# A two-direction gated recurrence: two score buffers, the output products moved behind the next tile's second group, and both directions' outputs in the same banks

## The reference

```python
S_t = diag(f_t) S_{t-1} + k_t v_t^T
o_t = S_t^T q_t
o   = o_forward + flip(o_backward)      # then an RMS norm for each head
```

## Time and profile before

| | |
|---|---|
| median of 3 runs | 4069.83 us (4064.1 to 4074.27) |
| the profiled execution | 4068.36 us |
| its span in the trace | 4066.5 us, mean granted PE clock 0.955 |
| PE busy | 3695.6 us, 91% of the span |
| DVE, ACT, POOL busy | 2607.3, 2022.8, 1042.4 us |

### The profile page before, as it was taken

The page is one execution under the profiler, slowest core; times in us unless marked ns, Lnnn a source line. Parts: engine busy times, 40 slices in busy tenths (PEclk is TensorE's granted clock), DMA queues, the critical chain, the costliest instruction groups (busy, mean ns, idle before and its releaser), DMA issues. The chain is left out here.

```text
span 4066.5 us, 57429 instructions
## 1 busy us (share of the span) xinstructions
PE 3695.6 (91%) x21576; PEld 2898.5 (71%) x21576; DVE 2607.3 (64%) x3794; ACT 2022.8 (50%) x3880; POOL 1042.4 (26%) x1106
## 2 busy tenths in 40 slices
PE   6999898888999787888789999999898989999998
PEld 5775677777775676767466666678666768888886
DVE  3766567767765486776555555548966776665655
ACT  4544366655544286655344444456644554444444
POOL 0016103732017003610155555500281010111000
PEclk7989899999989898999899999999999999999999
DMA  5100113345200102351100000122003551111344
GB/s 192 42 16 1 39 52 112 129 154 189 69 21 1 54 21 99 119 182 54 31 5 7 9 6 6 36 81 80 9 5 138 189 154 42 60 44 42 110 155 150
DMA packets 211397, 295.44 MB, mean 73 GB/s; under 512 B 74218, under 2 KB 140010, under 8 KB 211124
## 3 DMA queue, kind: packets, MB, share of 16 engines
q1 hardware_dynamic: 210564, 291.57, 21.6%
q0 software_dynamic: 416, 0.05, 0.0%
q10 hardware_dynamic: 144, 0.15, 0.0%
HBM read 261.12 MB, written 30.51 MB: 72 GB/s over the span
## 5 line engine op out<-in xcount | busy, mean ns | idle before, releaser
L563 DVE TENSOR_TENSOR x_low<-buf_a,x_high 128x640 fp32r<-128x640 f32 (+5 forms) x360 | 359.9, 1000 | 307.3 <-ACT x_high L610 290.2
L610 ACT CAST x_high<-buf_a 128x640 fp32r<-128x640 f32 (+5 forms) x360 | 311.0, 864 | 394.8 <-PE ps L670 322.2
L668 PE MATMUL ps<-x_high,w_high 128*128 128x512 f32 (+1 forms) x1184 | 443.4, 375 | 61.5 <-DVE w_low L567 55.9
L669 PE MATMUL ps<-x_low,w_high 128*128 128x512 f32 (+1 forms) x1184 | 436.9, 369 | 0.0
L670 PE MATMUL ps<-x_high,w_low 128*128 128x512 f32 (+1 forms) x1184 | 436.0, 368 | 0.0
L3321 PE MATMUL ps<-w_high,x_high 128*128 128x512 f32 x896 | 362.4, 404 | 53.9 <-DVE w_low L3170 52.0
L3322 PE MATMUL ps<-w_low,x_high 128*128 128x512 f32 x896 | 356.1, 397 | 0.0
L3323 PE MATMUL ps<-w_high,x_low 128*128 128x512 f32 x896 | 355.7, 397 | 0.0
L3170 DVE TENSOR_TENSOR w_low<-w,w_high 128x1024 fp32r<-128x1024 f32 x170 | 226.4, 1332 | 172.7 <-ACT w_high L3262 172.7
L3905 DVE TENSOR_REDUCE mx<-ps 128x1 fp32r<-128x1280 f32 x128 | 190.7, 1491 | 200.2 <-PE ps L3780 199.7
L668 PEld LDWEIGHTS ps<-x_high,w_high 128*128 128x128 f32 x1184 | 226.6, 191 | 109.7 <-DVE x_low L563 64.6
(11 more groups left out here) (451 smaller groups left out, 8910.9 us busy)
## 6 DMA issues: line engine op xcount, KB each, us to landing
w<-in_w_out SPq DMA_DIRECT2D x26, 2048.0 KB, 8.4
w<-in_w_mod SPq DMA_DIRECT2D x24, 2048.0 KB, 9.1
w<-in_w_down SPq DMA_DIRECT2D x15, 2048.0 KB, 7.9
w<-in_w_in SPq DMA_DIRECT2D x26, 1024.0 KB, 5.2
w<-in_w_up SPq DMA_DIRECT2D x22, 1024.0 KB, 7.6
w<-in_w_in SPq DMA_DIRECT2D x6, 2048.0 KB, 8.8
x<-in_x SPq DMA_DIRECT2D x16, 512.0 KB, 8.9
scratch_h<-x SPq DMA_DIRECT2D x8, 512.0 KB
```

The lines of the kernel that those rows point to most:

```text
L563: dve.tensor_tensor(part(xl, i)[:, 0:s["tn"]], x_of(s), part(xh, i)[:, 0:s["tn"]].bitcast(F32), ALU.subtract).then_inc(x_low, 1)
L610: act.copy(part(xh, i)[:, 0:s["tn"]], x_of(s)).then_inc(x_high, 1)
L668: pe.matmul(g["out"], lhs[0][:, :], rhs[0][:, :], start=(s["kk"] == 0), stop=False)
L669: pe.matmul(g["out"], lhs[0][:, :], rhs[1][:, :], start=False, stop=False)
```

## The change

- `sc` becomes two buffers for each direction, taken in turn by tile. `place` then waits only for the output product of two tiles ago. Two more buffers are cleared at the start.
- The four blocks of outputs get columns of their own for each direction in banks 6 and 7 (`r.out`). The first direction's first product alone carries `start`. The two directions' output products no longer wait for each other, but both readers (`first_output`, `output`) wait for the products of both directions, and the next tile's products wait for both readers.
- On PE `outputs_of(r, u-1)` moves from ahead of group 0 to behind group 1 of the same direction. Turned keys and state products come after both directions' level products.
- On DVE `output` moves from group 0 to the end of group 2, and `state` behind both directions' copies of group 1.
- On ACT `first_output` moves to the end of group 1, `squares` from group 2 to group 3, and the first modulation copy-out from the end of the tile to the end of group 2. Both `place` come ahead of both `keys_out`.

```diff
@@ scalar
-                act.wait_ge(r.o_ready, j) if j else act.wait_ge(r.zeroed, 2)
+                act.wait_ge(r.o_ready, j - 1) if j >= 2 else act.wait_ge(r.zeroed, 3)
...
-                act.wait_ge(r.o_ready, n_out[u] + 1)
+                for w in D2:
+                    act.wait_ge(w.o_ready, n_out[u] + 1)
...
                     for r in D2:
                         if g == 0:
-                            if u:
-                                first_output(r, u - 1)
                             place(r, u)
+                    for r in D2:
+                        if g == 0:
                             keys_out(r, u)
                         if g == 1 and u + 1 < NU:
                             exponentials(r, u + 1)
                         if first <= u < NU - 1:
                             level_exponentials(r, u + 1, g)
-                        if g == 2 and u:
+                        if g == 1 and u:
+                            first_output(r, u - 1)
+                        if g == G - 1 and u:
                             squares(r, u - 1)
-                for j in mods_at.get(u, ()):
+                    if g == 2:
+                        for j in mods_at.get(u, ())[:1]:
+                            mods.evacuate(act, mods.first + j)
+                for j in mods_at.get(u, ())[1:]:
                     mods.evacuate(act, mods.first + j)
@@ vector
                     for r in D2:
-                        if g == 0 and n_out[u]:
-                            output(r, u - 1)
                         copies(r, u, g)
                         if g == 0:
                             scale_levels(r, u, G - 1)
                         elif u + 1 < NU:
                             scale_levels(r, u + 1, g - 1)
+                    for r in D2:
                         if g == 1:
                             state(r, u)
+                        if g == 2 and n_out[u]:
+                            output(r, u - 1)
@@ tensor
-                if r is D2[1]:
-                    pe.wait_ge(D2[0].o_out, j + 1)
-                elif j:
+                if r is D2[0] and j:
+                    pe.wait_ge(D2[0].o_out, j)
                     pe.wait_ge(D2[1].o_out, j)
...
                     for r in D2:
-                        if g == 0 and n_out[u]:
+                        level_products(r, u, g)
+                        if g == 1 and n_out[u]:
                             outputs_of(r, u - 1)
-                        level_products(r, u, g)
+                    for r in D2:
                         if g == 0:
                             turn_keys(r, u)
                         if g == 1:
                             states(r, u)
@@ Scan
-        self.sc = lay("sc" + n, [P, 2, 2, P])
+        self.sc = [lay(f"sc{n}{i}", [P, 2, 2, P]) for i in range(2)]
+        self.out = slice(direction * P, (direction + 1) * P)
```

More of the change, by code:

```diff
@@ L1094, in place @@
                 act.wait_ge(r.products, G * j + 1)
-                act.wait_ge(r.o_ready, j) if j else act.wait_ge(r.zeroed, 2)
-                to = r.sc[:, :, :, :].rearrange("p a c t -> p (a c) t")
+                act.wait_ge(r.o_ready, j - 1) if j >= 2 else act.wait_ge(r.zeroed, 3)
+                to = r.sc[j % 2][:, :, :, :].rearrange("p a c t -> p (a c) t")
                 heads = ps[:, r.bank:r.bank + 2, :].rearrange("p a (c x) -> p (a c) x", c=2)
@@ L1117, in first_output @@
                     return
-                act.wait_ge(r.o_ready, n_out[u] + 1)
-                src = ps[:, 6:8, 0:P].rearrange("p a (c e) -> p a c e", c=2)
+                for w in D2:
+                    act.wait_ge(w.o_ready, n_out[u] + 1)
+                src = ps[:, 6:8, r.out].rearrange("p a (c e) -> p a c e", c=2)
                 act.copy(o[:, r.order[u], :].rearrange("p (c a e) -> p a c e", c=2, a=2), src).then_inc(r.o_out, 1)
@@ L1211, in output @@
                 j, t = n_out[u], r.order[u]
-                dve.wait_ge(r.o_ready, j + 1)
-                src = ps[:, 6:8, 0:P].rearrange("p a (c e) -> p a c e", c=2)
+                for w in D2:
+                    dve.wait_ge(w.o_ready, j + 1)
+                src = ps[:, 6:8, r.out].rearrange("p a (c e) -> p a c e", c=2)
                 dst = o[:, t, :].rearrange("p (c a e) -> p a c e", c=2, a=2)
@@ L1220, in _ @@
             for r in D2:
-                dve.memset(r.sc[:, :, :, :], 0.0).then_inc(r.zeroed, 1)
+                for sc in r.sc:
+                    dve.memset(sc[:, :, :, :], 0.0).then_inc(r.zeroed, 1)
                 dve.memset(r.S[0][:, :, :], 0.0).then_inc(r.zeroed, 1)
-                dve.wait_ge(r.zeroed, 2)
+                dve.wait_ge(r.zeroed, 3)
             for r in D2:
@@ L1291, in outputs_of @@
                 pe.wait_ge(r.qe_scaled, j + 1)
-                if r is D2[1]:
-                    pe.wait_ge(D2[0].o_out, j + 1)
-                elif j:
+                if r is D2[0] and j:
+                    pe.wait_ge(D2[0].o_out, j)
                     pe.wait_ge(D2[1].o_out, j)
                 for h in range(4):
-                    c, out = h // 2, ps[:, 6 + h % 2, h // 2 * HD:(h // 2 + 1) * HD]
-                    pe.matmul(out, r.sc[:, h % 2, c, :], v[:, t, h * HD:(h + 1) * HD], start=(c == 0), stop=False,
-                              skip_group_check=True)
+                    c, out = h // 2, ps[:, 6 + h % 2, r.out.start + h // 2 * HD:r.out.start + (h // 2 + 1) * HD]
+                    pe.matmul(out, r.sc[j % 2][:, h % 2, c, :], v[:, t, h * HD:(h + 1) * HD],
+                              start=(c == 0 and r is D2[0]), stop=False, skip_group_check=True)
                 for h in range(4):
-                    c, p0, out = h // 2, (h % 2) * HD, ps[:, 6 + h % 2, h // 2 * HD:(h // 2 + 1) * HD]
+                    c, p0 = h // 2, (h % 2) * HD
+                    out = ps[:, 6 + h % 2, r.out.start + h // 2 * HD:r.out.start + (h // 2 + 1) * HD]
                     mm = pe.matmul(out, r.qe[j % 2][p0:p0 + HD, c, :], r.S[u % 2][p0:p0 + HD, c, :], start=False,
@@ L1495, in mixer_layer @@
     mods.begin(*MODS_IN[layer], lambda j: 4 + j % 2, Layout(k, A_B, A_B + 4 * T * 4), BR + P)
-    recurrence(k, qk, a, v, o, (stat, junk), range(nt0, NT), Layout(k, A_A, A_B), mods)
+    recurrence(k, qk, a, v, o, (stat, junk), range(nt0, NT), Rooms(Layout(k, A_A, A_B), lay), mods)
     return RecurrenceNorm(k, layer, o, stat, YT, nt0, Layout(k, A_A, A_B),
```

## The result

| | median of the runs | the profiled execution, its span | ratio to before, 95% interval |
|---|---|---|---|
| before, 20 runs | 4067.77 us (4059.33 to 4078.48) | 4068.36, 4066.5 us | |
| changed, 20 runs | 4077.31 us (4072.53 to 4091.51) | 4074.3, 4072.5 us | 1.0029 [1.0019, 1.0039] |

The forecast was 4086 us, 16 above the median then known. Measured are 9.5 us by the two medians, and about 12 by the ratio. That lies at the edge of what can be told from no change, 0.3%, and its sign is clear. The profiled execution of the changed kernel is one of its quicker ones, 3 us under its median, so the profile shows less of the loss than the runs have. Of the 6.0 us between the two spans, 0.8 lie in the recurrences and 5.2 outside them, in code that did not change; what that part does is taken up behind the experiments.

What follows compares the result with a forecast made beforehand. PE idling for DVE's masked copies, in a chain of 18.41 us a tile, was taken as the bound. -7 us at full clock and +23 for low clock gave +16 on 4069.8: 4086 us, range 4062 to 4108.

Steps and rivals of the forecast that it cites:

- Its own sign of being wrong: Profile after: a recurrence clock of 0.94 and more, late tiles of 18 us, or squares ending before POOL's last group.
- What PE waited for: First recurrence: PE waited 14.5 us ahead of output products for DVE's last masked copy, 16 times, 0.9 us each.
- The early tile: Tiles whose last outputs are first-writer outputs: anchor to anchor about 17.35 us against 18.41, 1.05 less.
- The idle between the groups 0: PE in early tiles: idles 1.3 us between the two groups 0, and 0.5 ahead of direction 0's.
- The late tile: Five second-writer tiles: squares behind POOL-released exponentials delay `place`, next anchor at 19.8 us against 18.13, 1.7 lost in each.
- Position 1's tile: Tile with a second modulation product, whose copy-out on ACT holds `place` back: its time stays as before.
- The ends: First tiles take 16.7 and 15.9 us against 21.8 and 21.4; last tiles 3.7 more each; -3.2 in all.
- The sum at full clock: Both recurrences: early tiles -9.2, late tiles -1.5 and +6.8, ends -3.2; in all -7 us, earlier low clock taken as gone.
- The clock: PE falls to low clock in five late tiles and the second recurrence's first tile: 6 x 3.9 = +23 us.
- The expectation on low clock in late tiles: Late tiles idle 1.2, 1.4 and 1.9 us within 7.3 us, so a clock fall in each of five.
- The rule of the Trainium skill: PE micro-idling between groups of matmuls can make the clock gate fall and recover repeatedly; with it the sum is positive.

Runs made afterwards that it cites:

- kernel 4: The changed kernel plus unread products on PE ahead of group 0, between the groups 0 and ahead of late tiles' group 1; 4062.7 us, ratio 0.9973.
- kernel 1: The changed kernel with ACT's squares one tile later, in group 1, so not ahead of `place`; 4059.57 us, ratio 0.9978.
- kernel 6: kernel 1 plus unread products on PE ahead of and between the groups 0; 4055.45 us, ratio 0.9963.
- kernel 5: The kernel before plus five unread products on PE ahead of direction 0's output product; 4063.47 us, ratio 0.9975.
- kernels 2: The kernel before with two score buffers for each direction and nothing else of the change; 4069.55 us, ratio 1.0003.
- kernel 3: The changed kernel with each direction's output products behind its group 0 in place of group 1; 4085.63 us, ratio 1.0046.
- kernel 8: kernel 3 plus seven unread products on PE ahead of group 0 of direction 0; 4057.91 us, ratio 0.9959.
- Kernel 9: kernel 1 with DVE's additions a tile later, in group 0, plus unread products ahead of and between the groups 0; 4090.38 us, ratio 1.0044.
- kernel 10: kernel 8 with DVE's additions moved from the end of group 2 to the end of group 0; 4056.9 us, ratio 0.9955.

## Why the prediction was right

The direction held, and so did the reason, that idle between short products brings low clock which outweighs what the order gains; the size was 4 to 6 us too large. The profile is less kind to it. Its own sign of being wrong, a granted clock of 0.94 and more in the recurrence, is what the profile after shows (0.94 and 0.95), where it wanted less than 0.90, so the reason rests on the runs with filler and on the clocks of all executions. By its steps:

- **What PE waited for.** The 14.5 us ahead of the output products are those of both recurrences; the prediction read them as the first one's. Nothing in its sum uses them.
- **The early tile**, 17.35 predicted: 17.39. With the clock held (kernel 4) six of the eight take 17.4 and two 17.8, which was not looked into. DVE's two last copies end at 807.60 and 810.17, the groups 0 follow 0.1 later, and they start 13.1 and 15.7 after the anchor, as worked out (13.1 and 15.6).

```profile
806.10 1.50 DVE L1205 COPY_PREDICATED sc<-masks,ps 128x256 f32<-128x256 uint32 x2 [0.15 <-issue]
...
808.69 1.48 DVE L1205 COPY_PREDICATED sc<-masks,ps 128x256 f32<-128x256 uint32 x2
```

- **The idle between the groups 0**, 1.3 predicted: 1.34 to 1.41. Ahead of group 0 of direction 0 it was 0.5 predicted and 0.99 measured, because the products of group 3 end earlier than I had them; it moves no anchor, but it is twice the idle that the argument on the clock assumed in early tiles.
- **The late tile**, 19.8 predicted: 19.24 to 19.42 without a long stretch at low clock. The term is 0.4 too large because POOL's chain took 8.3 us, not 8.7; the rest, squares that hold `place` back, is as in the step. Kernels 1 and 6 show it: without the squares there, 17.7. Position 1's tile, which was to stay as it was (18.9 us, with a stretch at low clock in it), took 18.36.
- **The ends.** First tiles: 16.7 and 15.9 predicted, 16.64 and 16.06 measured. From the last anchor of the first recurrence to its end: 19.6 predicted, 871.19 - 850.58 = 20.6 measured, of which part is 2.0 us at low clock in the last output products.
- **The sum at full clock.** -7 us, with the low clock of before taken as gone, against 378.6 us for both recurrences: 371.6. Kernel 4, the changed order with its clock held, took 371.2. That the two are so near is partly luck: its early tiles are 1.3 us longer in sum than predicted, its late ones 2.6 shorter, and its first tile 0.7 longer. Of these -7 some 6 are no merit of the order, since the prediction's sum had taken the falls of before as gone: kernel 5 shows that the kernel before reaches 372.5 when its clock holds in all tiles but the first.
- **The clock.** +23 predicted, as six stretches at 3.9 us, one in each of the five late tiles and one in the first tile of the second recurrence. By the runs with and without filler it is 21 to 23, but the agreement is luck in good part. Of the six places, two had a stretch in or just behind them in the first profile of the changed kernel and three in the second; the first tile of the second recurrence had none in either, and early tiles had one or two. A short stretch (3.4 us) costs 1.5 us, spread over two tiles (18.64 + 18.09 in place of kernel 4's 17.40 + 17.82), or nothing under the squares, and a long one (10.2 us) costs 4.4 (23.84 against 19.42). In the kernel before, a long one costs 3.6 and not 3.9, since position 2's tile takes 18.4 at full clock (kernels 2 and 5) and not 18.1. The profiled executions of the changed kernel account for 379.4 - 371.2 = 8 us and 382.3 - 371.2 = 11 us; the rest lies in executions that were not profiled, whose granted clock is lower, and outside the two recurrences. There the same code took 3686.9 to 3694.0 us in the executions profiled, with 302 to 327 us of it at low clock; most of those with more low clock are the longer ones. Why it varies there was not traced.
- **Why +12 and not +16.** -7 and the 21 to 23 give +14 to +16, and the ratio with its interval +8 to +16, so the difference lies within what the terms are known to. In the -7 the low clock of before stands for about 6 us, as its one profile has it; by kernel 5 it cost 10. With 10 there, the sum is +10 to +12.
- **The expectation on low clock in late tiles** held in part: two and three of the five late tiles had a stretch. The rule of the Trainium skill that the prediction weighed against the sum ("TensorE: Matmul & The Clock Gate", section "A second HAM failure mode: psum-queue depth-cycling", on micro-idling between groups of matmuls) agrees with the filler runs. The prediction's remark that before shows falls after idles of under 1 us holds for two of its three; the one at 703.9 came after 1.02 us. What the rule would not have told is kernel 3, which idles less ahead of its level products than the changed kernel and lost more.

Several of the experiments' expectations failed. Kernel 1 was expected to gain little beyond its tile time and gained 20 us: the price of the squares had left out the clock. Kernel 3 was expected near 4061 and ran at 4086 for the same reason; kernel 8 settles it. Kernels 4 and 5 gained 21 to 23 and 10 us where 8 to 15 and 4 to 8 were expected, and kernel 6 some 6 us over kernel 1 by the ratios, as its rival had it, though the intervals overlap: low clock was underrated each time. Kernel 9 was expected to be the best and lost by its own wait, and kernel 10's 2 to 4 us over kernel 8 did not show in the whole, though its late tiles fell as expected. What stays open is why an idle of 1.0 to 1.7 us brings a fall in one tile and none in the next, and what ends a stretch. That output products keep the clock low once it has fallen is only suggested: every stretch of 10 us looked at holds them, and those of 3.4 us in the changed kernel lie between them.

## What to carry to other kernels

Moving work out from behind a wait gains only up to the next chain: here 1.0 us a tile of the up to 3 that moving the products could have given, and the squares, placed behind an instruction that waits for POOL, cost 1.6 us a tile where the next tile's copy was queued behind them. Where PE idles about a microsecond between short products, compare two orders only with the clock held, by a few products that nobody reads, and look at the granted clock of every execution: without them the order of kernel 3 looked 0.46% slower, with them it was 0.41% faster. Such filler must wait for nothing that comes later in another engine's list than the work it stands ahead of.

## What the runs showed of the hardware

- The granted clock fell to 0.50 in or after idle stretches of 0.94 to 1.69 us between short products, and not after all of them; at the end of a recurrence it fell some 2.2 us behind one of 0.69 us. Once low it stayed so for about 3.4, 6.8, 10.2, 13.7 or 17.1 us, and these lengths came back from one kernel to the next.
- Products that nobody reads made kernels faster: 5 a tile by 10 us (the one before), 14 or 22 by 21 to 23 us (the changed one), 7 by 35 us (kernel 3).
- With them, executions of the changed kernel lay 5 us apart in place of 19, and of the one before 7 in place of 19; but those of kernels 6 and 10 still lay 15 and 14 us apart. The scatter goes with the granted clock: in the changed kernel from 0.954 at 4072.8 us to 0.949 at 4091.5.
